# A top-k search moved out of attention units into a transposes stage

## The chip, the cores and the metric

The kernel runs on one core of a Trainium2 chip. The metric is the device time of one execution in microseconds (us). The engines are named by what they are: TensorE (PE in the rows; PEld is its weight load), VectorE (DVE), ScalarE (ACT), GpSimd (POOL) and SyncE (SP), which here only issues transfers. The core's matmul results lie in PSUM, of which the kernel uses eight banks of 128 x 512 fp32.

## The reference, cut to what matters

The model has two blocks of two layers each, over 512 tokens of width 1024. The change touches the second block alone. Each of its layers projects the tokens to queries and keys of three kinds of attention and to the operands of an index:

```python
moba = moba_attention(qk(mq, ...), qk(mk, ...), mv)          # 4 heads of 64
diff = diff_attention(dq_h[:, 0::2], dq_h[:, 1::2],          # (softmax(q1k1) - lam * softmax(q2k2)) v
                      dk_h[:, 0::2], dk_h[:, 1::2], dv, lam) # 4 pairs of heads
dsa = dsa_attention(qk(sq, ...), qk(sk, ...), sv, iq_h, ik_r, iw)
```

The third kind attends only to keys that an index picks:

```python
score = jnp.einsum('bch,bhcs->bcs', iwc, jax.nn.relu(logits))
score = jnp.where(kpos[None, :] <= qpos[:, None], score, -jnp.inf)
_, sel = lax.top_k(score, n_top)        # n_top = min(256, S // 4) = 128
```

So for each query the 128 largest index scores are wanted, and dsa attention needs them; moba and diff attention don't.

## The kernel before, in words

Tokens lie in `T` = 4 tiles of 128 partitions. A stage is one block of the program: each engine has its own instruction list in it, and the engines meet at its end before the next begins. For a layer of the second block the stages are the projection (`second_projection_stage`), the q/k transposes (`transpose_stage` with the name "qk_t"), the attention (`pair_attention_stage`), the transposes of its result, and the output projection with the feed-forward part.

**The search.** The index scores of token tile t are a row of (t + 1) x 128 columns in the tile `proj`. Tile 0 has only 128 keys and needs no search, so the search runs over tiles 1, 2, 3 with rows of 256, 384 and 512 columns. A step on a tile finds the eight largest values of each row (MAX8) and overwrites them by -3e38 (a match-value load and a MATCH_REPLACE8). A round is a step on each of the three tiles; 16 rounds find 128 values. Each result is followed by a wait of VectorE on its own semaphore (`Link`). The projection stage runs 16 - LATE = 8 rounds (`find_top`, L3122 and L3125), all three MAX8 first and then all three replaces, with one link after each group. The other 8 rounds are 24 single steps in the attention stage, one per unit, `IndexSearch.step` calling `take` (L2897, L2898), with a link after the MAX8 and one after the replace. In unit 24, `step` then writes the three masks (L2906), for which TensorE waits (`search.masked`) ahead of the dsa units with a mask.

**The q/k transposes.** There are 16 jobs. In each, TensorE transposes four 128 x 128 blocks into one bank (L274), and one engine copies the bank, 128 x 512, to the tile `qk_t`: ScalarE the even jobs (L288), VectorE the odd ones (L304 as a copy, L306 with the scale of the queries). A job waits for the copy of the job eight before it.

**The attention units.** `pairs` lists 32 units in the order diff (16), moba (8), dsa (8). Unit i has token tile i mod 4 and so nk = 128, 256, 384 or 512 keys; a unit holds two heads. All engines run a software pipeline over i, in this order of instructions within a turn:

- TensorE: two score products of unit i (L3251) and the mask product (L3254), after the exps of unit i - 2; the transposes of the probabilities of unit i - 2 (L3267); the product with v of unit i - 3 (L3280).
- VectorE: the negated row maximum of unit i over both heads (`tensor_reduce`, L3293); for a diff unit i - 1 the reciprocal, the ratio and the merge of its two softmaxes (L3299 to L3302); the search step; for a moba or dsa unit i - 4 the reciprocal and the scaled output (L3311, L3314).
- ScalarE: the scaled output of a diff unit i - 4 (L3325), the copy of the transposed probabilities of unit i - 2 (L3334), the two exps of unit i with their sums (L3342). In turns 20 to 24 it also computes squares and a root for the norm of the diff output (`DiffEnd`).

A diff unit merges its two softmaxes into one matrix, so one transposed copy and one product follow; moba and dsa units keep two. SyncE loads weights of the next stages ahead during the attention.

Of the kernel before, what the change touches and what calls it, by code (L numbers as in the profile page):

```python
# [26 lines left out]
T = S // P  # L27
# [4 lines left out]
NBANK = 8  # L32
# [38 lines left out]
HD = 64  # L71
# [4 lines left out]
N_TOP = min(256, S // 4)  # L76
# [174 lines left out]
    return nc.tensor.matmul(out, a, b[1], start=False, stop=stop, **more)  # L251


def transpose_stage(env, stage, jobs, ahead=None):

    nc, ps, ident = env.nc, env.ps, env.ident
    pairs = isinstance(jobs[0][1], tuple)
    turned = env.sem(stage, "turned")  # L260
    act_copied, dve_copied = env.sem(stage, "act_copied"), env.sem(stage, "dve_copied")

    with nc.Block() as block:  # L263
        @block.tensor
        def _(pe):
            for i, (srcs, dst, scale) in enumerate(jobs):
                if i >= NBANK:
                    if pairs:
                        pe.wait_ge(dve_copied, i - NBANK + 1)
                    else:  # L270
                        pe.wait_ge(dve_copied if i % 2 else act_copied, (i - NBANK) // 2 + 1)
                for j, src in enumerate(srcs):
                    w = src.shape[1]
                    last = nc.tensor.transpose(ps[0:w, i % NBANK, j * P:(j + 1) * P], src, ident)  # L274
                last.then_inc(turned, 1)

        def bank(eng, i):
            srcs, dst, scale = jobs[i]
            eng.wait_ge(turned, i + 1)
            return ps[0:srcs[0].shape[1], i % NBANK, 0:len(srcs) * P], dst, scale  # L280

        @block.scalar
        def _(act):
            if ahead is not None:
                env.stream.split_hi(act, ahead)
            for i in range(0, len(jobs), 1 if pairs else 2):
                src, dst, scale = bank(act, i)
                nc.scalar.activation(dst[0] if pairs else dst, src, ACT.Copy if scale is None else ACT.Identity,  # L288
                                     scale=1.0 if scale is None else scale).then_inc(act_copied, 1)

        @block.vector
        def _(dve):
            for i in range(0 if pairs else 1, len(jobs), 1 if pairs else 2):
                src, dst, scale = bank(dve, i)
                if pairs:
                    dve.wait_ge(act_copied, i + 1)
                    hi = dst[0].bitcast(F32)
                    if scale is None:
                        ins = nc.vector.tensor_tensor(dst[1], src, hi, ALU.subtract)
                    else:  # L300
                        ins = nc.vector.scalar_tensor_tensor(out=dst[1], in0=src, scalar=scale, in1=hi,
                                                             op0=ALU.mult, op1=ALU.subtract)
                elif scale is None:
                    ins = nc.vector.tensor_copy(dst, src)  # L304
                else:
                    ins = nc.vector.tensor_scalar(dst, src, scale, None, ALU.mult)  # L306
                ins.then_inc(dve_copied, 1)

        if ahead is not None:
            @block.sync  # L310
            def _(sp):
                env.stream.load(sp, ahead + env.stream.RAW + 1)

            @block.gpsimd
            def _(pool):
                env.stream.split_lo(pool, ahead)
# [2426 lines left out]
def pair_tile(nc, ctx, name, *shape, side="left"):  # L2743

    return tuple(ctx.enter_context(nc.sbuf_tensor(f"{name}_{n}", [P, *shape], F32R, side=side, allow_name_mangling=True)) for n in ("hi", "lo"))
# [128 lines left out]
def index_score(proj, t):  # L2874

    return proj[:, t, B_IQ:B_IQ + (t + 1) * P]


class IndexSearch:

    TAKEN, ROUNDS, LATE = -3e38, N_TOP // 8, 8

    def __init__(self, env, ctx, proj):
        self.env, self.proj = env, proj
# [8 lines left out]
    def take(self, link, t):  # L2895
        v, score = self.env.nc.vector, index_score(self.proj, t)
        link(v.max(self.top[:, t, :], score))  # L2897
        link(v.match_replace(score, self.top[:, t, :], score, self.TAKEN))  # L2898

    def step(self, dve, link, i):  # L2900

        if i < self.LATE * len(self.tiles):
            self.take(link, self.tiles[i % len(self.tiles)])
        if i == self.LATE * len(self.tiles):
            for t in self.tiles:
                self.env.nc.vector.tensor_scalar(self.mask(t)[0], index_score(self.proj, t), self.TAKEN, MASKED,  # L2906
                                                 ALU.not_equal, ALU.mult).then_inc(self.masked, 1)
# [16 lines left out]
def second_layer_units(base=0):  # L2924

    units, jobs = second_projection_units(base)
    first_out = base + len(units)
    units += weight_units("w_out_2", D, 0, D)
    first_ffn = base + len(units)
    for c in range(0, D_FF, F_CH):  # L2930
        units += [(w, 0, D, c, c + F_CH) for w in ("w_gate_2", "w_up_2")]
    units += weight_units("w_down_2", D_FF, 0, D)
    return units, jobs, first_out, first_ffn
# [417 lines left out]
def second_layer(env, l, dram, x, y, rows, base, vec2, gains, small, out, saved):  # L3351
# [3 lines left out]
    units, jobs, first_out, first_ffn = second_layer_units(base)  # L3355

    with ExitStack() as local:
        def tile(ctx, name, *shape):
            return ctx.enter_context(nc.sbuf_tensor(name, [P, *shape], F32, allow_name_mangling=True))

        with ExitStack() as mix:
            assert l or -(-nc.sbuf_base // 32) * 32 == env.entry_at
            proj = tile(mix, "proj2", T, IN2)
# [3 lines left out]
            diff_gain = tile(mix, "diff_gain", 1)  # L3367
            with ExitStack() as pre:
                ht = pair_tile(nc, pre, "attn_ht", KD, S)
                room = tile(pre, "index_room", IDX_H // 2 + 3, S) if l else y.rearrange("p t (i s) -> p (t i) s", i=2)  # L3370
                chunk = [room[:, i, :] for i in range(IDX_H // 2 + 3)]
                entry = Entry(env, pre, "proj2", x, ht, (lambda t: proj[:, t, B_DQ:B_DQ + D]) if l else env.entry_loads.landing,
                              None if l else (y, env.entry_loads), gains[:, 0:KD], True)
                second_projection_stage(env, entry, [] if l else early_units(base), chunk[0:IDX_H // 2 + 1], chunk[IDX_H // 2 + 1:],
                                        jobs, proj, vec2, iw, lam[:, 0:1], gains[:, 2 * KD:2 * KD + 1],
                                        diff_gain[:, 0:1], IndexSearch.LATE)
            rows.close()
            with ExitStack() as heads:

                qk_t = tile(heads, "qk_t", 16, S)  # L3380
                cols = ([B_MQ + c * P for c in range(4)] + [B_DQ + c * P for c in range(8)]
                        + [B_SQ + c * P for c in range(4)])
                is_q = [True, True, False, False] + [True] * 4 + [False] * 4 + [True, True, False, False]
                transpose_stage(env, "qk_t", [([proj[:, t, c:c + P] for t in range(T)], qk_t[:, n, :],
                                               HD ** -0.5 if is_q[n] else None) for n, c in enumerate(cols)])
                search = IndexSearch(env, heads, proj)

                def half(chunk, side, a, b):
                    return qk_t[side * HD:(side + 1) * HD, chunk, a:b]

                pairs = []
                for name, n_pairs, q0, k0, v0, y0, w in (("diff", 4, 4, 8, B_DV, B_DQ, 2 * HD),
                                                         ("moba", 2, 0, 2, B_MV, B_MQ, HD), ("dsa", 2, 12, 14, B_SV, B_SQ, HD)):
                    for n in range(n_pairs):
                        for t in range(T):
                            nk = (t + 1) * P
                            merge = name == "diff"
                            vs = [v0 + n * P + h * w for h in range(1 if merge else 2)]
                            pairs.append(dict(
                                merge=merge, nk=nk, q=[half(q0 + n, h, t * P, nk) for h in range(2)],  # L3400
                                k=[half(k0 + n, h, 0, nk) for h in range(2)],
                                v=[[proj[:, b, c:c + w] for b in range(t + 1)] for c in vs],
                                dst=proj[:, t, y0 + n * P:y0 + (n + 1) * P],
                                mask=search.mask(t) if name == "dsa" and t in search.tiles else None))
                diff_end = DiffEnd(env, heads, proj[:, :, B_DQ:B_DQ + 512])
                pair_attention_stage(env, "attn2", pairs, lam[:, 0:1], search, diff_end, first_out + 3)
# [172 lines left out]
```

## Time and profile before

| | us |
|---|---|
| median of 3 runs | 2596.79 |
| lowest and highest | 2595.59, 2601.40 |
| the profiled execution, its own time | 2597.38 |
| span of its instructions | 2595.6 |

In the span TensorE is busy for 2391.2 us, VectorE for 1752.6, ScalarE for 1318.1 and GpSimd for 614.4. The first layer's transposes stage stands at 1380 to 1388 us of the span and its attention stage from 1388 to about 1485; those of the second layer stand at 2081 and 2089. Times in the rows are counted from the span's start. A busy share is the part of a stretch in which an engine executes something; the granted clock is the share of full speed that TensorE was given.

### The profile page before, as it was taken

To read this page: it belongs to the slowest core of one execution; us is meant where nothing else is said; L and a number is where in the kernel's file an instruction comes from. 1 tells how busy PE (TensorE), PEld (TensorE's weight loads), DVE (VectorE), ACT (ScalarE), POOL (GpSimd) and SP (SyncE) were. 2 spreads that over 40 slices of the span, in tenths; PEclk is the share of its full clock that TensorE was granted. 3 is DMA by queue.
4 is the path that set the end of the run, shared out by engine and by line. 5 is a ranking of instruction groups with operands and counts; after the bars stand their busy time and mean duration, and the time that the engine had idled before them with its cause. 6 is when DMAs were issued, how large, how long until landed. Compare 5 with 4: busy or idle time off the path is not lost. (4 is left out here: it accounts for less than half of the span.)

```text
span 2595.6 us, 37232 instructions
## 1 busy us (share of the span) xinstructions
PE 2391.2 (92%) x14216; PEld 2015.2 (78%) x14216; DVE 1752.6 (68%) x2747; ACT 1318.1 (51%) x2638; POOL 614.4 (24%) x337
## 2 busy tenths in 40 slices
PE   7999896997999896996998899999999989999999
PEld 7866675776866775775786789998887857899987
DVE  1755757874655756876698669995256985699942
ACT  3446625773546615775655744444157456444421
POOL 2401304771401303782360110000023501100000
PEclk9999987998999987998998999999999999999999
DMA  4210027983210017993120023323222201123221
GB/s 161 81 39 1 1 99 288 353 331 125 83 49 1 1 58 285 349 335 135 66 98 17 5 91 118 111 82 106 85 91 73 91 1 48 72 102 116 100 87 72
DMA packets 54994, 285.84 MB, mean 110 GB/s; under 512 B 13216, under 2 KB 13216, under 8 KB 28704
## 3 DMA queue, kind: packets, MB, share of 16 engines
q1 hardware_dynamic: 45600, 266.65, 28.1%
q0 software_dynamic: 9216, 16.80, 1.7%
q8 instruction: 114, 1.87, 0.3%
q14 instruction: 64, 0.52, 0.1%
HBM read 275.02 MB, written 25.17 MB: 116 GB/s over the span
## 5 line engine op out<-in xcount | busy, mean ns | idle before, releaser
L229 POOL TENSOR_TENSOR weights_lo<-weights_raw,weights_hi 128x2048 fp32r<-128x2048 f32 (+4 forms) x53 | 239.2, 4515 | 729.7 <-issue 358.6
L240 PE MATMUL ps<-x_operands,weights_hi 128*128 128x256 f32 x1232 | 347.7, 282 | 5.8 <-DVE weights_lo L1945 5.1
L241 PE MATMUL ps<-x_operands,weights_hi 128*128 128x256 f32 x1232 | 348.8, 283 | 0.0
L242 PE MATMUL ps<-x_operands,weights_lo 128*128 128x256 f32 x1232 | 348.2, 283 | 0.0
L215 ACT ACTIVATE weights_hi<-weights_raw 128x2048 fp32r<-128x2048 f32 (+5 forms) x86 | 148.2, 1723 | 307.9 <-PE ps L242 288.4
L240 PEld LDWEIGHTS ps<-x_operands,weights_hi 128*128 128x128 f32 x1232 | 233.7, 190 | 8.4 <-DVE weights_lo L1945 6.8
L242 PEld LDWEIGHTS ps<-x_operands,weights_lo 128*128 128x128 f32 x1232 | 231.7, 188 | 0.0
L241 PEld LDWEIGHTS ps<-x_operands,weights_hi 128*128 128x128 f32 x1232 | 231.0, 187 | 0.0
L240 PE MATMUL ps<-weights_hi,attn_ht_hi 128*128 128x512 f32 (+2 forms) x576 | 204.7, 355 | 4.3 <-DVE weights_lo L229 2.3
L241 PE MATMUL ps<-weights_lo,attn_ht_hi 128*128 128x512 f32 (+2 forms) x576 | 201.2, 349 | 0.0
L242 PE MATMUL ps<-weights_hi,attn_ht_lo 128*128 128x512 f32 (+2 forms) x576 | 200.5, 348 | 0.0
L229 DVE TENSOR_TENSOR weights_lo<-weights_raw,weights_hi 128x2048 fp32r<-128x2048 f32 (+3 forms) x33 | 65.1, 1973 | 179.6 <-ACT weights_hi L215 179.6
L240 PE MATMUL ps<-weights_hi,x_operands 128*128 128x512 f32 x384 | 152.9, 398 | 6.2 <-PEq L263 6.2
L241 PE MATMUL ps<-weights_lo,x_operands 128*128 128x512 f32 x384 | 152.9, 398 | 0.0
L240 PE MATMUL ps<-weights_hi,xt_hi 128*128 128x480 f32 (+2 forms) x384 | 138.9, 362 | 5.8 <-DVE weights_lo L229 2.5
L1939 ACT ACTIVATE weights_hi<-ffn_w_sums 128x1024 fp32r<-128x1024 f32 x66 | 70.0, 1060 | 133.4 <-DVE ffn_w_sums L2249 133.4
L242 PE MATMUL ps<-weights_hi,xt_lo 128*128 128x480 f32 (+2 forms) x384 | 136.1, 354 | 0.0
L241 PE MATMUL ps<-weights_lo,xt_hi 128*128 128x480 f32 (+2 forms) x384 | 135.8, 354 | 0.0
L240 PEld LDWEIGHTS ps<-weights_hi,attn_ht_hi 128*128 128x128 f32 x576 | 110.1, 191 | 28.0 <-issue 9.1
L242 PE MATMUL ps<-weights_hi,ffn_hidden_lo 128*128 128x512 f32 x320 | 125.8, 393 | 0.0
L242 PEld LDWEIGHTS ps<-weights_hi,attn_ht_lo 128*128 128x128 f32 x576 | 109.9, 191 | 13.4
L241 PEld LDWEIGHTS ps<-weights_lo,attn_ht_hi 128*128 128x128 f32 x576 | 110.2, 191 | 11.7
(531 smaller groups left out, 6259.5 us busy)
## 6 DMA issues: line engine op xcount, KB each, us to landing
weights_raw<-in_stream SPq DMA_DIRECT2D x96, 1024.0 KB, 4.7
weights_raw<-in_expert_gu SPq DMA_DIRECT2D x34, 1024.0 KB, 9.5
expert_raw<-in_expert_gu SPq DMA_DIRECT2D x30, 1024.0 KB, 9.7
expert_raw<-in_expert_down SPq DMA_DIRECT2D x18, 1024.0 KB, 8.5
weights_raw<-in_expert_down SPq DMA_DIRECT2D x14, 1024.0 KB, 8.2
weights_raw<-in_stream SPq DMA_DIRECT2D x12, 960.0 KB, 4.5
ffn_raw<-in_stream SPq DMA_DIRECT2D x10, 1024.0 KB, 4.8
weights_raw<-in_stream SPq DMA_DIRECT2D x8, 700.0 KB, 9.5
```

What stands on the lines that cost most here:

```text
L215: self.nc.scalar.activation(self.split_tiles(u)[0][:, 0:n], self.env.raw[:, u % self.RAW, 0:n], ACT.Copy).then_inc(self.hi_ready, 1)
L229: eng.tensor_tensor(lo[:, 0:n], self.env.raw[:, u % self.RAW, 0:n], hi[:, 0:n].bitcast(F32), ALU.subtract).then_inc(self.lo_ready, 1)
L240: nc.tensor.matmul(out, a[0], b[0], start=start, stop=False, **more)
L241: nc.tensor.matmul(out, a[0], b[1], start=False, stop=False, **more)
L242: return nc.tensor.matmul(out, a[1], b[0], start=False, stop=stop, **more)
L1939: nc.scalar.activation(ring(g)[0], quarter(c, w_of[p]), ACT.Copy).then_inc(w_hi_done, 1)
```

## The change

`transpose_stage` takes an argument `vector_work`. With it, ScalarE copies all jobs, TensorE waits for ScalarE's copies alone, and VectorE runs the given function in the stage. For "qk_t" that function is the new `IndexSearch.rounds`: BESIDE = 3 rounds in the form of the projection stage's. LATE goes from 8 rounds to 5, and the projection keeps 16 - (5 + 3) = 8. The 15 single steps that remain in the attention stage are taken in the units that the new `light` names: those with i mod 4 < 2 among the diff units, and all from unit 16 on. They fall in units 0, 1, 4, 5, 8, 9, 12, 13 and 16 to 22, and the masks are written in unit 23.

```diff
-def transpose_stage(env, stage, jobs, ahead=None):
+def transpose_stage(env, stage, jobs, ahead=None, vector_work=None):
...
+                    elif vector_work is not None:
+                        pe.wait_ge(act_copied, i - NBANK + 1)
...
-            for i in range(0, len(jobs), 1 if pairs else 2):
+            for i in range(0, len(jobs), 1 if pairs or vector_work is not None else 2):
...
         @block.vector
         def _(dve):
+            if vector_work is not None:
+                vector_work(dve)
+                return
...
-    TAKEN, ROUNDS, LATE = -3e38, N_TOP // 8, 8
+    TAKEN, ROUNDS, LATE, BESIDE = -3e38, N_TOP // 8, 5, 3
...
+    def rounds(self, dve):
+
+        link = Link(dve, self.env.sem("index", "vector_step"))
+        v = self.env.nc.vector
+        for _ in range(self.BESIDE):
+            for t in self.tiles:
+                last = v.max(self.top[:, t, :], index_score(self.proj, t))
+            link(last)
+            for t in self.tiles:
+                score = index_score(self.proj, t)
+                last = v.match_replace(score, self.top[:, t, :], score, self.TAKEN)
+            link(last)
+
+    def light(self, i):
+
+        return i >= 4 * T or i % T < 2
+
     def step(self, dve, link, i):
 
-        if i < self.LATE * len(self.tiles):
-            self.take(link, self.tiles[i % len(self.tiles)])
-        if i == self.LATE * len(self.tiles):
+        if not self.light(i):
+            return
+        n = sum(self.light(j) for j in range(i))
+        if n < self.LATE * len(self.tiles):
+            self.take(link, self.tiles[n % len(self.tiles)])
+        if n == self.LATE * len(self.tiles):
...
-                                        diff_gain[:, 0:1], IndexSearch.LATE)
+                                        diff_gain[:, 0:1], IndexSearch.LATE + IndexSearch.BESIDE)
...
+                search = IndexSearch(env, heads, proj)
                 transpose_stage(env, "qk_t", [([proj[:, t, c:c + P] for t in range(T)], qk_t[:, n, :],
-                                               HD ** -0.5 if is_q[n] else None) for n, c in enumerate(cols)])
-                search = IndexSearch(env, heads, proj)
+                                               HD ** -0.5 if is_q[n] else None) for n, c in enumerate(cols)],
+                                vector_work=search.rounds)
```

## Rows read from the trace of the kernel before

**Rows 1.** The page: span, and TensorE's busy time, share and instructions.
```profile
span 2595.6 us, 37232 instructions
...
PE 2391.2 (92%) x14216; PEld 2015.2 (78%) x14216; DVE 1752.6 (68%) x2747; ACT 1318.1 (51%) x2638; POOL 614.4 (24%) x337
```

**Rows 2.** By stretch: length, then busy us of PE, PEld, DVE, ACT, POOL; granted clock, DMA.
```profile
1388.00:1404.00 16.00, 14.74 (x58) 9.66 (x58) 14.09 (x37) 9.23 (x30) 0.00 (x0) 0.57 0.00 1
1404.00:1437.00 33.00, 26.31 (x156) 18.15 (x156) 30.90 (x80) 19.98 (x69) 0.00 (x0) 0.91 0.00 1
...
2100.00:2138.00 38.00, 31.03 (x177) 21.97 (x176) 36.16 (x93) 22.56 (x78) 0.00 (x0) 0.87 0.00 1
```

**Rows 3.** Waits, 1388 to 1437 and 1437 to 1480 us: total, times, longest.
```profile
DVE attn_top L3293 <- PE ps L3254: 1.8, 2, 1.2
...
DVE attn_top L3293 <- PE ps L3254: 14.3, 10, 2.5
```

**Rows 4.** VectorE's timeline: steps, reduces of unit 0 and unit 17, both layers.
```profile
1389.11 0.42 DVE L3293 TENSOR_REDUCE attn_top<-ps 128x2 f32<-128x256 f32 x1 [1.22 <-PE ps L3254]
...
1407.20 0.42 DVE L2897 MAX8 index_top<-proj 128x8 f32<-128x256 f32 x1
...
1408.17 1.22 DVE L3293 TENSOR_REDUCE attn_top<-ps 128x2 f32<-128x1024 f32 x1
...
1410.30 0.55 DVE L2897 MAX8 index_top<-proj 128x8 f32<-128x384 f32 x1
...
1411.54 0.42 DVE L3293 TENSOR_REDUCE attn_top<-ps 128x2 f32<-128x256 f32 x1
...
1413.00 0.69 DVE L2897 MAX8 index_top<-proj 128x8 f32<-128x512 f32 x1
...
1414.51 0.69 DVE L3293 TENSOR_REDUCE attn_top<-ps 128x2 f32<-128x512 f32 x1
...
1437.44 0.69 DVE L3293 TENSOR_REDUCE attn_top<-ps 128x2 f32<-128x512 f32 x1
...
2089.87 0.43 DVE L3293 TENSOR_REDUCE attn_top<-ps 128x2 f32<-128x256 f32 x1 [1.22 <-PE ps L3254]
...
2137.54 0.69 DVE L3293 TENSOR_REDUCE attn_top<-ps 128x2 f32<-128x512 f32 x1
```

**Rows 5.** Timeline of the transposes stage: start us, duration us, engine, line.
```profile
1378.99 0.69 ACT L649 ACTIVATE proj<-ps,proj_entry 128x512 f32<-128x512 f32 x1 [2.06 <-PE ps L242]
...
1379.99 7.18 PE L274 MATMUL ps<-consts,proj 128*128 128x128 f32 x64 [1.03 <-PEq L2980]
1380.65 0.60 ACT L288 ACTIVATE qk_t<-ps 128x512 f32<-128x512 f32 x1 [0.97 <-PE ps L274]
...
1387.20 0.69 DVE L304 COPY qk_t<-ps 128x512 f32<-128x512 f32 x1 [0.18 <-PE ps L274]
1388.18 1.28 ACT L3342 ACT_TABLE_LOAD   x1 [0.81 <-PEq L263]
```

**Rows 6.** VectorE's timeline, projection stage: first round of three, next work.
```profile
1358.01 1.42 DVE L3122 MAX8 index_top<-proj 128x8 f32<-128x256 f32 x3
...
1367.62 0.29 DVE L3073 TENSOR_TENSOR rope_tables<-consts,vec 128x128 f32<-128x128 f32 x1
```

**Rows 7.** ScalarE's timeline: two copies from PSUM in a row.
```profile
1460.36 1.06 ACT L3334 ACTIVATE attn_prob_t<-ps 128x512 f32<-128x512 f32 x2
```

**Rows 8.** Timeline: unit 3's reduce, step and exp end; TensorE's scores, units 2, 6.
```profile
1396.22 1.23 DVE L3293 TENSOR_REDUCE attn_top<-ps 128x2 f32<-128x1024 f32 x1
...
1398.34 0.42 DVE L2897 MAX8 index_top<-proj 128x8 f32<-128x256 f32 x1
...
1398.73 0.20 ACT L3342 ACTIVATION_READ_ACCUMULATOR attn_prob<-ps,attn_top 128x1 f32 x1
...
1390.43 1.65 PE L3251 MATMUL ps<-qk_t 64*128 64x384 f32 x4 [0.35 <-ACT attn_prob L3342]
...
1404.09 0.92 PE L3251 MATMUL ps<-qk_t 64*128 64x384 f32 x4
```

## The prediction

> **What bounds the kernel now.** I read the page first: one core, a span of 2595.6 us, TensorE busy for 92% of it [rows 1]. That average says nothing of the stretch that the change touches, so I went on to busy time by stretch. The first layer of the second block has its q/k transposes at 1380 to 1388 us and its 32 attention units from 1388 to about 1485; the second layer repeats both 700 us later. In the stretch of the diff units VectorE is busy 14.09 of 16 us and 30.90 of 33 us, and most of the rest is issue gaps inside its own queue [rows 2]. The table of waits says it more sharply: from 1388 to 1437 us VectorE waits for scores 1.8 us in all, 1.2 of them before the first unit; from 1437 on, 14.3 us in ten waits [rows 3]. So VectorE sets the pace of units 0 to 16, and the TensorE/ScalarE chain that of the later ones.
>
> The timeline gives the price of a search step there. From one MAX8 to the next unit's reduce: 0.97 us for the 256-wide row, 1.24 for 384, 1.51 for 512 [rows 4]; three of them, one round, are 3.72 us. From the first reduce (1389.11) to that of unit 17 (1437.44) are 48.33 us; in the second layer 2089.87 to 2137.54, 47.67 us [rows 4]. Of this the 17 steps of units 0 to 16 (six, six and five of each width) are 6 x 0.97 + 6 x 1.24 + 5 x 1.51 = 20.81 us. The other 26.9 us are reduces and merges.
>
> **The transposes stage, where work is added.** Its 16 banks are now copied by both engines in turn. ScalarE's last store before it ends at 1378.99 + 0.69 = 1379.68; its own first copy begins at 1380.65; the last VectorE copy ends at 1387.20 + 0.69 = 1387.89, and the next stage's first instruction comes at 1388.18, 0.29 later [rows 5]. By the same 0.29, VectorE can begin its rounds at about 1379.97 instead of waiting for the first bank.
>
> A round in the new form, three MAX8, then three replaces with only two links, stands in the projection stage: three of them take 1367.62 - 1358.01 = 9.61 us [rows 6]. So VectorE would be through at 1379.97 + 9.61 = 1389.58, against 1387.89. ScalarE alone: two copies of 128x512 out of PSUM, back to back, last 1.06 us together, and one alone 0.60, so one follows another after 0.46 us [rows 5, 7]. Sixteen end at 1380.65 + 15 x 0.46 + 0.60 = 1388.2, under the rounds. TensorE fills a bank in 0.44 us (7.18 for 16, [rows 5]), so with eight banks it never waits for the copies. The scaled copies are of the same form and duration. The stage therefore grows by 1389.58 - 1387.89 = **+1.7 us** per layer. Bounds: it grows by 0.3 us if only the copies counted; if each copy of ScalarE cost 0.875 us, the spacing at which its copies start today when it takes every second bank, it would end at 1394.4, +6.5. I take the back-to-back row, as it is of the same shape and source.
>
> The Trainium skill (ScalarE: Activation LUTs, What ACT_TABLE_LOAD costs) gives 186 ns + 0.833 ns per element for an ACTIVATE with immediates and an overlap of 93 ns, so 0.52 us per copy, and the copies would end at 1389.0. The row of two copies says 0.46; by either the rounds end last, but by the skill the margin is 0.5 us instead of 1.4.
>
> **The diff units, where work goes.** Steps are now allowed in units 0, 1, 4, 5, 8, 9, 12, 13 and from 16 on. Up to unit 16 these are nine, three of each width: 3 x 3.72 = 11.16 us. Removed from VectorE's queue: 20.81 - 11.16 = **9.65 us** per layer.
>
> Not all comes back. Where VectorE's pace falls, it meets ScalarE. In unit 3 the reduce starts at 1396.22 and the read of the second exp's sum ends at 1398.73 + 0.20 = 1398.93, 2.71 us later [rows 8]. Without its step VectorE would reach the next merge earlier. From the reduce to the start of its step (0.97 us long) are 1398.34 - 1396.22 = 2.12 us, the reduce of unit 4 adds 0.34, so VectorE arrives 2.46 us after the reduce and waits 0.25 to 0.3 us. This comes once for each four units, four times: 1.2 us. Scores of the widest units may come some 0.2 us late once or twice. I take 1.5 us, so **-8.2 us** per layer. Below: no such waits, -9.65. Above: TensorE at half clock, next part.
>
> **TensorE's clock.** The granted clock is 0.57 over 1388 to 1404 us, that is mostly the lower of its two levels, 1.2 GHz, and 0.91 over 1404 to 1437; in the second layer 0.87 over 2100 to 2138 [rows 2]. Before the first fall TensorE had done its transposes and idled about a microsecond at the stage's switch. Today the fall costs almost nothing, since VectorE is slower still: the first layer's 48.33 us against the second's 47.67. But at the lower clock four units take TensorE 1404.09 - 1390.43 = 13.66 us [rows 8], while VectorE would now need (26.9 + 11.16) / 4 = 9.5 us. Each four units inside a slow stretch give back up to 13.7 - 9.9 = 3.8 us of the gain; and before, VectorE needed 11.9 of the 13.7 anyhow. A repeat of the long first stretch (about 13.6 us) costs 3.3 us in one layer; short ones, as those of the second layer, 0.2 to 1 us each. I take 3.3 + 1.2 = **+4.5 us** for both layers; bounds 0 (no stretch) and 8 (a long one in each layer, 2 x 3.3 + 1.2).
>
> The Trainium skill (Perfetto Trace Analysis, Matmul Optimizations) says that TensorE scales its power with use, so matmuls should come back to back. That speaks against the change: TensorE now stands idle from 1387.2 to about 1390, 2.8 us instead of 1.0. The trace agrees so far that a fall followed this switch in one layer of two. By the rule alone a long slow stretch would follow in both layers.
>
> **Later units.** The steps of units 17 to 22 change width (by 0.27 or 0.54 us), where VectorE waits 14.3 us in ten waits [rows 3] or ScalarE is full (squares, table loads). The masks move from unit 24 to 23, where a step of 1.51 goes; the next exp stands behind ScalarE's table loads. I take 0, bounds -1 and +1 for both layers. Nothing in the stages behind starts differently but earlier: no DMA is issued by the moved steps, the projection keeps its 8 rounds (5 + 3), and the DMA engines are near idle.
>
> **Sum.** Two layers: 2 x 1.7 - 2 x 8.2 + 4.5 = -8.5, say -9. The profiled execution took 2597.4 us, 1.8 above its span; the median of the runs is 2596.8, 0.6 below it. 2596.8 - 9 = **2588 us**, 0.35% faster. A measurement of this kernel can tell 0.2%, or 5.2 us, from no change.
>
> **The rivals.**
> (A) As forecast, VectorE's relief comes through less a clock term: 2583 to 2591.5. Chance 0.76.
> (B) ScalarE is the new bound of the transposes: 0.875 us per copy, a semaphore wait with each. Then the stage costs +6.5 per layer, and the sum is 2 x (6.5 - 8.2) + 4.5 = +1: 2598, no change. For it: its copies do start 0.875 apart today. Against: the waits between them are for TensorE, which had filled the bank of the other engine meanwhile. 0.07.
> (C) The slower side. TensorE falls to the lower clock at the longer idle switch and stays there through the diff units of both layers. Four groups of 13.66 are 54.6 us, 7 more than 47.7; with the longer transposes 2 x (7 + 1.7) = +17: 2614. It decides from the point where slow time exceeds about seven units per layer (6.5 us net over 3.8 per four units); the first layer spent 14 us so, four units. For it: the fall follows idle time. Against: the work is denser after the change, and the clock came back at 1404 by itself. 0.04.
> (D) The gain does not appear, since units without a step are bound by the exp-scores chain as closely as VectorE now is: if every unit without a step were bound as before, only half of it, 4 us per layer, came back: -8.2 + 3.4 + 4.5, about 0. Against: the waits table shows VectorE one wait of 0.6 us from unit 1 to unit 16 [rows 3]. 0.07.
> (E) Clock dips vanish altogether: 2596.8 - 13 - 1 = 2583 or less. 0.06.
>
> **Numbers.** Faster by over 0.2%: A and E, 0.82; within it: B and D, 0.14; slower: C, 0.04. The range 2582.5 to 2594 takes in E's edge, and goes up halfway to B and D.
>
> **What would show it.** In the trace after: sixteen ScalarE copies some 0.46 apart, MAX8 beginning before the first copy, and attention starting 1.7 us later after the transposes' start; first reduce to that of unit 17 in 39.5 us where the clock is 1.00, about 43 in a slow layer; VectorE waits of about 0.3 us at merges 3, 7, 11, 15. Wrong if copies are 0.6 or more apart, if VectorE waits for scores at every wide unit, or if the clock stays at 0.5.

## The result

| | us |
|---|---|
| before, median of 5 runs | 2596.79 |
| after, median of 5 runs (2582.42 to 2587.35) | 2583.64 |
| ratio, with its 95% interval | 0.9943 (0.9932 to 0.9955) |
| span of the profiled execution, before and after | 2595.6, 2581.0 |

The kernel is 0.57% faster. By the ratio that is 14.8 us, a time of 2582.0, just under the lower end of the forecast range (2582.5); the median is inside it. The forecast change was 9 us.

The profile after. The page first, then busy time by stretch with the columns of [rows 2]:

```profile
span 2581.0 us, 37216 instructions
...
PE 2384.1 (92%) x14216; PEld 2007.1 (78%) x14216; DVE 1740.0 (67%) x2731; ACT 1323.6 (51%) x2654; POOL 614.5 (24%) x337
```

```profile
1390.00:1404.00 14.00, 13.08 (x63) 7.88 (x63) 12.10 (x32) 9.11 (x32) 0.00 (x0) 0.76 0.00 1
1404.00:1420.00 16.00, 13.91 (x91) 9.44 (x89) 14.88 (x37) 11.73 (x43) 0.00 (x0) 1.00 0.01 2
1420.00:1437.00 17.00, 16.13 (x114) 11.88 (x114) 15.90 (x38) 12.91 (x46) 0.00 (x0) 1.00 0.00 1
...
2084.00:2090.00 6.00, 6.00 (x19) 2.95 (x19) 4.70 (x13) 2.65 (x11) 0.00 (x0) 0.50 0.01 3
2090.00:2124.00 34.00, 29.87 (x195) 20.72 (x194) 31.45 (x79) 25.21 (x88) 0.00 (x0) 1.00 0.00 1
```

The stretch of the diff units is 40 us long now, not 48. TensorE's clock is low in its first units only: 0.76 to 1404 us (0.57 in [rows 2]) and in the second layer 0.50 for six microseconds; after that it is 1.00 to the end of the diff units, where it was 0.87 and 0.91.

The timeline of the first layer's transposes stage and of the start of attention, answering to [rows 5] and the first of [rows 4]:

```profile
1379.21 1.48 DVE L2911 MAX8 index_top<-proj 128x8 f32<-128x256 f32 x3 [2.22 <-PEq L3005]
1379.22 7.18 PE L276 MATMUL ps<-consts,proj 128*128 128x128 f32 x64 [1.03 <-PEq L3005]
1379.89 7.95 ACT L290 ACTIVATE qk_t<-ps 128x512 f32<-128x512 f32 x16 [0.97 <-PE ps L276]
...
1388.18 0.68 DVE L2915 MATCH_REPLACE8 proj<-index_top,proj 128x512 f32<-128x512 f32 x1
1389.34 1.28 ACT L3367 ACT_TABLE_LOAD   x1 [1.51 <-PEq L263]
...
1389.38 0.49 PE L3276 MATMUL ps<-qk_t 64*128 64x128 f32 x4 [2.98 <-PEq L263]
...
1390.28 0.42 DVE L3318 TENSOR_REDUCE attn_top<-ps 128x2 f32<-128x256 f32 x1 [1.43 <-PE ps L3279]
```

VectorE's first MAX8 stands beside the first transpose. ScalarE's sixteen copies end at 1379.89 + 7.95 = 1387.84, the rounds at 1388.18 + 0.68 = 1388.86, and TensorE has idled for 2.98 us when the next stage starts.

For the account I cut each layer's stretch in three: S from the first transpose to the reduce of unit 0, D from there to the reduce of unit 17, L from there to that of unit 31.

| us | S | D | L |
|---|---|---|---|
| before, first and second layer | 9.12, 9.12 | 48.33, 47.67 | 40.20, 40.20 |
| after | 11.06, 11.46 | 40.18, 40.10 | 38.36, 38.36 |
| change of both | +4.3 | -15.7 | -3.7 |

The sum is -15.1; 0.2 more stand behind the last reduce and 0.3 elsewhere, and the spans differ by 14.6. The interval from reduce to reduce is the same to 0.02 us in either layer and in every kernel below, wherever steps and clock are the same. So these three numbers tell a few tenths of a microsecond, which the timed ratios (intervals of 0.3%, 8 us, for kernels timed in a few runs) do not. Only the places at which the clock falls differ: each profile is one execution, and what low clock it met, above all in D, is not a property of the kernel alone.

### The profile page after: what moved, and what is told of

Same layout as the page of the kernel before. It is cut to its first block and busy times, and to the rows that moved or that the text cites. A ratio compares the mean times of both kernels' runs of the same rounds, so it can differ in the third digit from the quotient of the medians.

```text
span 2581.0 us, 37216 instructions
## 1 busy us (share of the span) xinstructions
PE 2384.1 (92%) x14216; PEld 2007.1 (78%) x14216; DVE 1740.0 (67%) x2731; ACT 1323.6 (51%) x2654; POOL 614.5 (24%) x337
```

## The experiments

All kernels are the changed one with one edit. Two of them leave steps of the search out, as their expectations say.

**The parts of S.** ScalarE alone, nothing beside it, steps as before:

```diff
-    TAKEN, ROUNDS, LATE, BESIDE = -3e38, N_TOP // 8, 5, 3
+    TAKEN, ROUNDS, LATE, BESIDE = -3e38, N_TOP // 8, 8, 0
-        return i >= 4 * T or i % T < 2
+        return True
```

> ScalarE copies all 16 banks of q/k, VectorE does nothing in that stage, and the 24 single steps stand one in each of units 0 to 23 as before the change. Forecast's price (one copy after another at 0.46 to 0.50 us): from the first transpose to the first reduce 9.4 us instead of 9.1, whole kernel +0.6 us over the kernel before (2597). Rival B (0.875 us per copy): 15.6 us for the stage, +13 us (2610).

Ratio to the kernel before 1.0011 (1.0002 to 1.0021). S is 9.82 us in both layers, D 48.55 and 47.71, L 41.80 and 40.21 (a dip at unit 25 in the first layer). ScalarE's timeline in this kernel:

```profile
1382.52 7.95 ACT L290 ACTIVATE qk_t<-ps 128x512 f32<-128x512 f32 x16 [0.97 <-PE ps L276]
1390.73 1.28 ACT L3367 ACT_TABLE_LOAD   x1 [0.27 <-PEq L263]
```

Sixteen copies last 7.95 us, so one follows another after (7.95 - 0.60) / 15 = 0.49 us. That is the forecast's price and a little more (+0.7 us per layer, not +0.3); rival B with 0.875 us is dead.

Then the changed kernel with the three rounds left out and both engines copying:

```diff
-                                               HD ** -0.5 if is_q[n] else None) for n, c in enumerate(cols)],
-                                vector_work=search.rounds)
+                                               HD ** -0.5 if is_q[n] else None) for n, c in enumerate(cols)])
```

> The changed kernel with the three rounds in the transposes stage left out and both engines copying there as before: the search runs 13 of its 16 rounds. It shows the cost of the stage by itself: first transpose to first reduce 9.1 us instead of 11.1, attention as in the changed kernel, so 3.9 us less in all (2580). If the longer idle switch also costs clock, unit 0 to 17 falls to 39.6 us and it is 5 us less.

0.9910 (0.9894 to 0.9927). S is 9.12 again in both layers, so the stage costs 1.94 us (2.34 where the clock is low at the first scores). D is 40.81 and 41.69, not less, although the idle switch is short again: the clock falls all the same, only elsewhere (around unit 13 in both layers, at units 2 and 3 in the second).

**TensorE kept busy at the switch.**

```diff
+            if vector_work is not None:
+                for i in range(len(jobs), len(jobs) + 5):
+                    pe.wait_ge(act_copied, i - NBANK + 1)
+                    for j, src in enumerate(jobs[0][0]):
+                        nc.tensor.transpose(ps[0:src.shape[1], i % NBANK, j * P:(j + 1) * P], src, ident)
```

> The changed kernel with 20 more transposes on TensorE at the end of the q/k transposes stage (2.2 us, into banks that are already copied and are not read), so that TensorE is busy until VectorE's rounds end. If the idle time at the switch brings the clock down: the granted clock is 1.00 over the first 14 us of attention instead of 0.76, and unit 0 to 17 takes 39.6 us instead of 40.2: about 1 us less in all. If it is not the idle time: the same dips, no change.

0.9928 (0.9911 to 0.9944), which is not to be told from the changed kernel. TensorE's timeline, the added transposes and the mask products of units 0, 4, 5 and 6, whose duration shows the clock (0.44 us at full, 0.69 at half):

```profile
1387.82 2.35 PE L282 MATMUL ps<-consts,proj 128*128 128x128 f32 x20
...
1391.39 0.44 PE L3284 MATMUL ps<-exact 128*128 128x128 f32 x2
...
1398.62 0.44 PE L3284 MATMUL ps<-exact 128*128 128x128 f32 x2
...
1402.56 0.69 PE L3284 MATMUL ps<-exact 128*128 128x128 f32 x2
...
1406.50 0.44 PE L3284 MATMUL ps<-exact 128*128 128x128 f32 x2
```

The idle time fell from 2.98 to 0.80 us and units 0 to 4 ran at full clock, yet a dip came at unit 5; in the second layer it came at unit 4. So the clock falls without the long idle switch too, some 7 us later after the first reduce in both layers. D is 41.72 and 39.52: against the 39.28 us that the changed kernel's intervals add up to at full clock the dips cost 2.4 and 0.2 us, where those of the changed kernel cost 0.9 and 0.8. From two layers of one execution it isn't shown that a later dip is the dearer one.

**A step ahead of the first reduce.**

```diff
                 for i in range(N + 4):
+                    if i == 0:
+                        search.step(dve, link, i)
                     if i < N:
...
-                    search.step(dve, link, i)
+                    if i:
+                        search.step(dve, link, i)
```

> The changed kernel with the step of unit 0 ahead of the first reduce, in the 1.4 us in which VectorE waits for the first scores, not behind it. If that wait is free: first reduce as before at 11.1 us, unit 0 to 1 shorter by up to 0.9 us, the whole kernel 1 to 1.8 us under the changed one. If TensorE or ScalarE bounds the first units (the wait of 0.25 us before unit 1): no change.

0.9943 (0.9926 to 0.9959), a miss. S is 11.53 and 11.14, unit 0 to 1 takes 1.69 us instead of 1.52 and 1.85: the step delays the first reduce in one layer, and the units behind wait for TensorE's scores (1.27 us before unit 1). VectorE is not the bound there. D is 40.04 and 42.02, the second with a long dip over units 1 to 5.

**Which units are freed.** The steps in a row instead of in the chosen units:

```diff
-        return i >= 4 * T or i % T < 2
+        return True
```

> The changed kernel without the choice of units: the 15 steps stand in units 0 to 14, the masks in unit 15. By VectorE's sum, unit 0 to 17 takes 26.9 + 18.6 = 45.5 us instead of 40.2. Forecast (later units cost nothing): 17 to 31 stays 38.4, +10.6 us over the changed kernel (2594). New theory: without steps units 17 to 24 go 1 to 2 us faster per layer, 17 to 31 in 36.5 to 37.5 us, +7 to +8.5 us over the changed kernel (2591).

1.0009 (1.0000 to 1.0019): no gain at all. Three rounds left the attention, but D is 49.97 and 47.48 (the first with dips at units 5 and 13) and L 39.75 and 40.27. The steps that went are those of units 15 to 23. VectorE's timeline in the second layer, units 19 to 24, is that of an engine that waits:

```profile
2149.35 1.22 DVE L3318 TENSOR_REDUCE attn_top<-ps 128x2 f32<-128x1024 f32 x1 [1.61 <-PE ps L3279]
2150.99 0.42 DVE L3318 TENSOR_REDUCE attn_top<-ps 128x2 f32<-128x256 f32 x1 [0.42 <-PE ps L3279]
...
2153.51 0.69 DVE L3318 TENSOR_REDUCE attn_top<-ps 128x2 f32<-128x512 f32 x1 [1.70 <-PE ps L3279]
...
2156.91 0.96 DVE L3318 TENSOR_REDUCE attn_top<-ps 128x2 f32<-128x768 f32 x1 [2.31 <-PE ps L3279]
...
2160.31 1.22 DVE L3318 TENSOR_REDUCE attn_top<-ps 128x2 f32<-128x1024 f32 x1 [2.05 <-PE ps L3279]
...
2161.96 0.42 DVE L3318 TENSOR_REDUCE attn_top<-ps 128x2 f32<-128x256 f32 x1
```

Units 16 to 27 took 31.5 us with eight steps before, and take 31.0 here with none and 30.2 in the changed kernel with seven. Both 31.5 and 31.0 hold a dip of the clock at unit 17, for which 0.84 us is found below. So the eight steps of units 16 to 23 gave back 0.5 us. My expectation also left out the masks in unit 15, 0.8 us; with them VectorE's sum is 46.3, and unit 0 at the low clock adds 0.5 (1.85 us for 1.31).

Then the long rows' units instead of the short ones:

```diff
-        return i >= 4 * T or i % T < 2
+        return i >= 4 * T or i % T >= 2
```

> The changed kernel with the eight steps of the diff units in units 2, 3, 6, 7, 10, 11, 14, 15 (long rows) instead of 0, 1, 4, 5, ... . By VectorE's sum nothing changes but its waits: the wait of 0.2 us at each merge of a unit 3, 7, ... goes, and waits for scores in the short units without a step come (reduce of 0.34 and 0.61 us behind scores of 0.7 to 1 us): from unit 0 to 17 41 to 43 us instead of 40.2, the whole kernel +1 to +5 us over the changed one. If VectorE alone counted: no change.

0.9973 (0.9964 to 0.9983). D is 45.74 and 44.39, above what either side expected. VectorE's timeline, units 12 to 14 of the second layer:

```profile
2111.52 0.42 DVE L3318 TENSOR_REDUCE attn_top<-ps 128x2 f32<-128x256 f32 x1
...
2112.31 0.75 DVE L3327 SCALAR_TENSOR_TENSOR attn_prob<-attn_prob,attn_ratio 128x512 f32<-128x512 f32 x1
2112.97 0.68 DVE L3318 TENSOR_REDUCE attn_top<-ps 128x2 f32<-128x512 f32 x1
...
2115.69 0.96 DVE L3318 TENSOR_REDUCE attn_top<-ps 128x2 f32<-128x768 f32 x1 [1.32 <-PE ps L3279]
```

With steps in units 10 and 11, VectorE is late with the merge of the 512-wide unit; TensorE's transposes and product of that unit, then the scores of unit 14, follow in its order, and VectorE has nothing to do for 1.32 us. The same number of steps in the short units falls into time that VectorE would otherwise wait.

All eight steps of the diff units left out:

```diff
-        return i >= 4 * T or i % T < 2
+        return i >= 4 * T
-        n = sum(self.light(j) for j in range(i))
+        n = 8 + sum(self.light(j) for j in range(i))
```

> The changed kernel without the eight steps of the diff units: they are left out, so the search is short of them. It tells what bounds the diff units once VectorE is freed. VectorE's own sum from unit 0 to 17 is 26.9 + 1.5 = 28.4 us. If VectorE were still the bound: 30 to 31 us. If the chain exp, scores, reduce, exp over two units bounds: 36 to 37.5 us, so that the last eight steps cost 3 us only and moving more of them brings little.

0.9930 (0.9914 to 0.9947), which is not to be told from the changed kernel with its steps. D is 41.39 and 39.10, above the 36 to 37.5 that I expected; the first layer has a dip of 13.65 us. The chain is the bound, here in units 8 to 16 of the second layer:

```profile
2102.73 0.42 DVE L3318 TENSOR_REDUCE attn_top<-ps 128x2 f32<-128x256 f32 x1
...
2104.91 0.69 DVE L3318 TENSOR_REDUCE attn_top<-ps 128x2 f32<-128x512 f32 x1 [0.35 <-PE ps L3279]
...
2107.25 0.96 DVE L3318 TENSOR_REDUCE attn_top<-ps 128x2 f32<-128x768 f32 x1 [0.94 <-PE ps L3279]
...
2109.70 1.23 DVE L3318 TENSOR_REDUCE attn_top<-ps 128x2 f32<-128x1024 f32 x1 [0.65 <-PE ps L3279]
...
2111.82 0.42 DVE L3318 TENSOR_REDUCE attn_top<-ps 128x2 f32<-128x256 f32 x1
...
2120.92 0.42 DVE L3318 TENSOR_REDUCE attn_top<-ps 128x2 f32<-128x256 f32 x1
```

Four units take 2111.82 - 2102.73 = 9.09 us, with three waits for scores and one of 0.20 for the exp; in the changed kernel, 9.66 us and the one wait of 0.20:

```profile
2102.61 0.42 DVE L3318 TENSOR_REDUCE attn_top<-ps 128x2 f32<-128x256 f32 x1
2103.23 0.17 DVE L3324 RECIPROCAL attn_recip<-attn_total 128x2 f32<-128x2 f32 x1 [0.20 <-ACT attn_prob L3367]
...
2105.60 0.69 DVE L3318 TENSOR_REDUCE attn_top<-ps 128x2 f32<-128x512 f32 x1
...
2108.43 0.96 DVE L3318 TENSOR_REDUCE attn_top<-ps 128x2 f32<-128x768 f32 x1
...
2110.15 1.22 DVE L3318 TENSOR_REDUCE attn_top<-ps 128x2 f32<-128x1024 f32 x1
...
2112.27 0.42 DVE L3318 TENSOR_REDUCE attn_top<-ps 128x2 f32<-128x256 f32 x1
...
2121.38 0.42 DVE L3318 TENSOR_REDUCE attn_top<-ps 128x2 f32<-128x256 f32 x1
```

These are the four units with the widest steps, 384 and 512. The next four, with steps of 256 and 384, take 9.11 us against 9.10, so there the steps cost nothing; units 4 to 7 take 9.53 against 9.09. The first four take 8.55 against 8.56, in both kernels with 6.8 us of low clock that began 1.1 us ahead of the first reduce. So the eight steps cost 40.10 - 39.10 = 1.0 us per layer, where VectorE's sum says 9.65, and the next step moved out would bring next to nothing. That is what the fourth round shows:

```diff
-    TAKEN, ROUNDS, LATE, BESIDE = -3e38, N_TOP // 8, 5, 3
+    TAKEN, ROUNDS, LATE, BESIDE = -3e38, N_TOP // 8, 4, 4
-        return i >= 4 * T or i % T < 2
+        return i >= 4 * T or i % T == 0 or i == 1
```

> The changed kernel with four rounds beside the copies and three steps fewer in the diff units (steps in 0, 1, 4, 8, 12). The stage grows by one round, 3.2 us, to 14.3 us. Unit 0 to 17 by VectorE's sum 3.7 us less, with the chain of the units 1 to 2 us less: the whole kernel 2 to 4 us over the changed one; by VectorE's sum alone 1 us under it.

0.9954 (0.9937 to 0.9971). S is 14.83 and 14.84, D 39.66 and 40.95: 3.4 to 3.8 us more per layer for 0.5 less at best. The stage's three rounds are about the right number.

**The later units.** Three kernels take L = 38.36 back to 40.20 piece by piece. The rows' order of units 16 to 22 as before:

```diff
-            self.take(link, self.tiles[n % len(self.tiles)])
+            self.take(link, self.tiles[(0, 1, 2, 0, 1, 2, 0, 2)[n] if i < 4 * T else i % len(self.tiles)])
```

> The changed kernel with the steps of units 16 to 22 on the rows that they had before the change (384, 512, 256, 384, 512, 256, 384 wide instead of 512, 256, 384, 512, 256, 384, 512). Forecast: no change in units 17 to 31. New theory (VectorE sets the pace in units 16, 17, 19 and 20 too): from unit 0 to 17 0.3 us less, from 17 to 31 0.8 us more (0.54 in 17, 0.54 in 20, 0.27 less in 19), so about +0.5 us per layer, +1 us in all.

0.9948 (0.9932 to 0.9965). In the second layer L is 38.76, +0.40: the wider rows in units 17 and 20 come back whole (0.54 us each), the narrower ones take off 0.27 in 18, 0.27 in 19, 0.12 in 21 and nothing in 22. In the first it is 39.60, with a dip of the clock at unit 17: 0.84 for the dip alone. The masks alone, back in unit 24:

```diff
-        if n == self.LATE * len(self.tiles):
+        if i == 4 * T + 8:
```

> The changed kernel with the masks written in unit 24 again, so that unit 23 has neither step nor masks. Forecast (ScalarE's table loads set the pace there): no change, 17 to 31 stays 38.4 us. New theory (VectorE still sets the pace between units 23 and 24, while its wait of 1.6 us before unit 25 covers the masks): unit 23 to 24 shorter by 0.6 to 0.8 us, the whole kernel 1.2 to 1.6 us under the changed one (2582).

0.9935 (0.9919 to 0.9952), L 38.37 and 38.36. Unit 23 is shorter by 0.71 and units 24 to 26 longer by 0.69: neither the masks nor their place costs anything, the forecast's view, and my new one of them was wrong. Last the step of unit 23 with the masks in 24, all later units as before the change:

```diff
-        return i >= 4 * T or i % T < 2
+        return i >= 4 * T or i % T < 2 and i != 13
-            self.take(link, self.tiles[n % len(self.tiles)])
+            self.take(link, self.tiles[n % len(self.tiles) if i < 4 * T else i % len(self.tiles)])
```

> The changed kernel with the search of units 16 to 24 exactly as before the change (a step in each of units 16 to 23 on the old rows, masks in 24); unit 13 has no step in turn. It tells what makes units 17 to 31 take 38.4 us instead of 40.2. Theory: the rows' order costs 0.4, the step of unit 23 0.6, and the rest, 0.85, is a fall of the clock at unit 17, which belongs to the diff units before it, not to the steps: 39.3 us here with the clock at full speed at unit 17. If the steps themselves were the cause: 40.2 us. Unit 0 to 17 shorter by 0.5 to 1.2 us.

0.9958 (0.9942 to 0.9975). L is 39.33 and 39.35, as expected; D is 39.96 and 41.77, with dips up to unit 3 and at unit 13 in the second layer, where I had expected it shorter. From 38.76 that is 0.58 for unit 23's step; what is left to 40.20 is 0.86. In the kernel before, TensorE's mask product for unit 17 takes 0.69 us, for unit 18 0.44:

```profile
1433.90 0.55 PE L3267 MATMUL ps<-consts,attn_prob 128*128 128x128 f32 x3 [2.18 <-DVE attn_prob L3302]
...
1436.01 0.69 PE L3254 MATMUL ps<-exact 128*128 128x128 f32 x2
...
1439.35 0.44 PE L3254 MATMUL ps<-exact 128*128 128x128 f32 x2
```

The dip stands there in both layers, behind a wait of 2.2 us for the merge of unit 14, whose transposes stand between the scores of units 16 and 17. VectorE's timeline after the change, from unit 17, with [rows 4] for before; the reduce of unit 18 before is put first:

```profile
2140.00 0.96 DVE L3293 TENSOR_REDUCE attn_top<-ps 128x2 f32<-128x768 f32 x1 [0.38 <-PE ps L3254]
```

```profile
2124.64 0.69 DVE L3318 TENSOR_REDUCE attn_top<-ps 128x2 f32<-128x512 f32 x1
...
2126.22 0.96 DVE L3318 TENSOR_REDUCE attn_top<-ps 128x2 f32<-128x768 f32 x1
...
2128.53 1.22 DVE L3318 TENSOR_REDUCE attn_top<-ps 128x2 f32<-128x1024 f32 x1 [0.23 <-PE ps L3279]
...
2131.18 0.42 DVE L3318 TENSOR_REDUCE attn_top<-ps 128x2 f32<-128x256 f32 x1
...
2132.91 0.68 DVE L3318 TENSOR_REDUCE attn_top<-ps 128x2 f32<-128x512 f32 x1
...
2136.03 0.96 DVE L3318 TENSOR_REDUCE attn_top<-ps 128x2 f32<-128x768 f32 x1 [0.80 <-PE ps L3279]
...
2139.43 1.23 DVE L3318 TENSOR_REDUCE attn_top<-ps 128x2 f32<-128x1024 f32 x1 [0.53 <-PE ps L3279]
...
2141.78 0.41 DVE L3318 TENSOR_REDUCE attn_top<-ps 128x2 f32<-128x256 f32 x1
```

Unit 17 takes 1.58 us; before it was 2.46 (2137.54 to 2140.00) with a wait. With the old rows and full clock it is 2.12 (second layer of the kernel with the rows' order as before), with the old rows and a dip 2.43 (its first layer).

**A try at a better split.**

```diff
-    TAKEN, ROUNDS, LATE, BESIDE = -3e38, N_TOP // 8, 5, 3
+    TAKEN, ROUNDS, LATE, BESIDE = -3e38, N_TOP // 8, 6, 2
...
+        self.take(link, self.tiles[2])
...
-        if n < self.LATE * len(self.tiles):
+        if n < 5 * len(self.tiles):
             self.take(link, self.tiles[n % len(self.tiles)])
-        if n == self.LATE * len(self.tiles):
+        if i == 21:
+            self.take(link, self.tiles[0])
+        if i == 23:
+            self.take(link, self.tiles[1])
+        if i == 24:
```

> A try at a better split: two rounds and one 512-wide step beside ScalarE's copies (7.9 us of VectorE, as long as the copies), the other two steps of the third round added to units 21 (256 wide) and 23 (384 wide), masks in 24. First transpose to first reduce 9.8 us instead of 11.1 to 11.5, unit 0 to 17 unchanged at 39.5 to 40.2, 17 to 31 longer by 0.5 to 0.9: 0.4 to 0.8 us less per layer, about 1 us under the changed kernel. If VectorE sets the pace in units 21 and 23, the two steps come back whole (2.2 us) and it is 1 us slower per layer.

0.9934 (0.9912 to 0.9957). S is 9.81 and 9.82, 1.25 under the changed kernel; L is 39.04, 0.7 over it. The 0.6 us per layer that are won are less than what the clock takes back in this execution (D 41.68 and 42.53, dips at units 2, 3 and 13 in the first layer, 2 to 5 in the second). It is not shown to be faster than the changed kernel. The low clock of its second layer, and that of the kernel with the step ahead of the first reduce, by the columns of [rows 2]:

```profile
2086.00:2100.00 14.00, 13.68 (x50) 8.93 (x50) 11.58 (x30) 8.02 (x29) 0.00 (x0) 0.51 0.01 1
```

```profile
2084.00:2098.00 14.00, 13.92 (x52) 8.77 (x51) 10.89 (x28) 7.69 (x27) 0.00 (x0) 0.51 0.00 1
```

## Why the prediction was off

The direction, the mechanism and the largest term held; two terms were wrong, both against the change. For both layers:

| us | forecast | measured |
|---|---|---|
| transposes stage | +3.4 | +4.3 |
| diff units at full clock | -16.4 | -16.8 |
| clock, diff units | +4.5 | +1.1 |
| later units | 0, bounds -1 and +1 | -3.7 |
| behind and elsewhere | 0 | +0.5 |

- **"The stage grows by 1.7 us per layer"**: the price of the rounds was right (9.65 us for 9.61, [rows 6]). The block switch took 0.48 us instead of the 0.29 of [rows 5], and in one layer the first scores ran at the low clock, 0.4 more. The sixteen copies took 7.95 us, 0.49 each. The figures of the Trainium skill (ScalarE: Activation LUTs, What ACT_TABLE_LOAD costs) make it an estimated 0.52 for each, so 8.4 us in all. The trace is below it, and by either number the rounds end last.
- **"So -8.2 us per layer"**: the intervals at full clock add up to 39.28 us for units 0 to 17, where I had 39.5; the four waits of 0.2 us for the exp are there. VectorE still sets the pace there, but by little: the chain that stands behind it takes 9.1 us per four units, and VectorE 9.53, 9.66 and 9.11 from unit 4 on.
- **"I take 3.3 + 1.2 = +4.5 us"** is the first failed step. I priced a repeat of the long first stretch of low clock. The changed kernel has one dip of 6.8 us per layer, in units 0 to 3, and pays 0.9 and 0.8 us against 39.28; the kernel before paid 0.66 in its first layer. The price of 3.3 us for a long stretch came out about right, though two of its inputs were misread and partly offset each other: the 13.66 us of [rows 8] hold waits for VectorE (the reduces of units 2 and 6 are 12.49 us apart), and (26.9 + 11.16) / 4 counts 17 units as 16. Two kernels with as many steps in the diff units, the step ahead of the first reduce and the better split, had such a stretch in the second layer (0.51 over 14 us). Their D is 42.02 and 42.53, 2.7 and 3.3 us over 39.28. So how long the clock stays low differs among kernels whose diff units are nearly the same, and part of the small +1.1 may be luck of the profiled execution: it is the second fastest of the five (2582.84 us, mean granted clock 0.962; the slowest took 2587.35 at 0.959), and where the clock fell in the others is not on record. Rival C, a clock that stays low, did not come near. The Trainium skill (Perfetto Trace Analysis, Matmul Optimizations) wants matmuls back to back, since TensorE's power goes with its use. The runs agree only in part: with the idle time at the switch filled down to 0.80 us the clock fell all the same, some 7 us later.
- **"Later units: I take 0"** is the second, and outside its bounds. I read 14.3 us of waits in ten waits [rows 3] as slack in every unit from 17 on. It is slack in 22 and in part in 21; in 17 to 20 a wider or narrower row shows in full. The order of rows brought 0.4 us and the step of unit 23 0.58 per layer. The largest part, 0.86, is the dip at unit 17, which I had missed because of the sentence **"Today the fall costs almost nothing, since VectorE is slower still"**. That holds inside the diff units. At unit 17 VectorE is no longer the bound, and each microsecond of slow TensorE counts. Its size is settled twice: 0.86 is left when rows, step and masks are put back, and 0.84 lies between the two layers of one kernel of which one has the dip.
- Why the dip at unit 17 went is argued, not shown. It stands in all six layers of the three kernels with a step in every diff unit up to 14 or later (before, ScalarE alone, steps in a row), and in one of the 20 layers of the ten kernels with steps at most in short units. TensorE's waits for a merge in the first layer's diff units were 7.4 us, the longest 2.2, and are 3.8, the longest 0.8. Their sum is not the cause: with the steps in the long rows' units they are 6.2 and 7.9 us, and neither layer has the dip. What goes with the dip is the wait for the merge of unit 14, just ahead of it: 1.9 to 2.2 us in those six layers, 1.3 us with the steps in the long rows' units, 0.7 or 1.0 us in the 20 others, the one with the dip among them. No run changed that wait by itself.
- Rival D is settled by the row of kernels: with no step in the diff units four units take 9.1 us. So the chain of exp, scores and reduce stood close behind VectorE, but where it stood before, at 11.3 to 11.9 us per four units from unit 4 on, VectorE alone was the bound, and 8.4 of the 9.65 us per layer came back.

## What to carry to other kernels

Ask of each piece of work not how long it is but in which turn it stands: the same eight steps cost 1.0 us in the short units and 5.3 in the long ones (D 40.10 and 44.39 against 39.10 with none, each with one dip of 6.8 us in its first units), and the eight taken from units 16 to 23 gave back 0.5 in units 16 to 27. A wait table over a stretch is a sum over turns with different bounds; read the intervals turn by turn before writing zero. A low clock costs nothing only up to the turn in which TensorE becomes the bound, so price it where the bound changes, in the kernel before too. Once the freed engine comes down to the next chain, here after three rounds, stop.

## What the runs showed of the hardware

TensorE's clock falls in each attention stage of each of these kernels at least once in the profiles, to 0.50 of full, for 3.4 to 17.1 us at a time. Filling its idle time at the switch from 2.98 to 0.80 us moved the fall by some 7 us and did not prevent it. A ScalarE copy of 128x512 from PSUM follows the one before after 0.49 us among the sixteen of the transposes and after 0.46 in the pair of [rows 7]. The program waits on a semaphore ahead of each copy in both places, so what makes the difference is not shown.
